# Modulation's first parts as six and two feature chunks, the first three units' products in another order, the input matrix turned later

## The chip, the cores and the metric

The kernel runs on one core of a Trainium2 chip, as one launch. Its time is the device time in microseconds (us), the median of several executions. All sizes are float32; the large products run as float32r, a form in which an operand is written as a high and a low part.

## The reference

Two transformer-like blocks over 512 tokens of 1024 features. The change touches only the beginning of the first block:

```python
def _rmsnorm(x, g):
    x32 = x.astype(jnp.float32)
    y = x32 * lax.rsqrt(jnp.mean(x32 * x32, axis=-1, keepdims=True) + EPS)
    return y.astype(x.dtype) * g
...
    c_act = jax.nn.silu(c)
    for l in range(DEPTH):
        mod = c_act @ w_ada[l] + b_ada[l]
        sh1, sc1, gt1, sh2, sc2, gt2 = jnp.split(mod, 6, axis=-1)
        u = _modulate(h, g_mix[l], sh1, sc1)
...
    proj = u @ w_in
    q, k, v, us, g_att, g_ssm = jnp.split(
        proj, [ATT_WIDTH, 2 * ATT_WIDTH, 3 * ATT_WIDTH, 3 * ATT_WIDTH + SSM_WIDTH,
               3 * ATT_WIDTH + SSM_WIDTH + D_MODEL], axis=-1)
```

The modulation vector `mod` is a product of one row with a 1024 x 6144 matrix. Its first two parts, the shift and the scale, are needed before the normalized input u can be formed, and u before any product with `w_in`. The state space branch (`us`) takes two of the first column blocks of `proj`; its input matrix B is scaled and grown over four steps before it is used. The rest of the reference, attention over three windows, gates, feed-forward parts and the whole second block, is the same before and after and does not bear on the change.

## The kernel before, in words

Activations lie transposed: 128 features on the partitions, 512 tokens along the row, so 1024 features are eight chunks. A **unit** is one block of 128 output columns: a weight tile of 128 x 1024 is loaded into `raw`, ScalarE (ACT) writes its high part `w_hi`, GpSimd (POOL) its low part `w_lo` (raw minus high), and TensorE (PE) makes for each of the eight chunks three products of 128x512 into one bank: high weights by high input, high weights by low input, low weights by high input, 24 in all. Two such buffers, s = 0 and 1, alternate for the whole kernel. ACT may refill a buffer's high part only when PE has signalled the end of the last unit that read it (`unit_done`); POOL follows ACT; PE waits for POOL (`lo_ready`).

Every engine runs a program written out by hand, in order, with semaphores between them; there is no scheduler. SyncE (SP) issues the loads.

The beginning goes like this. SP loads the columns, x, a table, then the first part of w_ada (shift and scale of chunks 0 to 3: eight loads of 512 KB, one for each 128 rows), three weight tiles of w_in, the second part (chunks 4 to 7), and so on. PE makes eight dummy products, then `ada_part(0, k)`: four quarter-array products for each of the eight loads, with dummy products (`keep_warm`) and two small sums for the norm between them. ACT copies the row out (`take_row`), PE turns it to columns (`turn_ada`), VectorE (DVE) makes shift and gain of four chunks (`take_half`), and then chunk by chunk: DVE scales x (`modulate`), ACT adds the shift and rounds (`shifted`, giving `u_hi`), DVE makes the rest (`shift_lo`, giving `u_lo`).

The first three units are not made one after the other, but grouped by chunk: `group_high`, `group_rest` and `group_low` are the three kinds of product for unit s and chunk c. Unit 2 has a place of its own (`third_raw`, `third_hi`, `third_lo`), units 0 and 1 use the two buffers. The second part's `ada_part(1, k)` stands between their products. After chunks 0 to 3 of all three come chunks 4 to 7 of units 0 and 1, then those of unit 2. Then PE turns the grown B matrix by 16 transposes of 128x128 (line 1068), which ACT copies out (line 1457), and the regular units begin with `in_unit` on buffer 1.

DVE grows B (`power_of_lam`, `grow`) between the first and second halves of its modulation, and POOL doubles a table of angles (`double`, `square_angle`) partly before, partly behind its first three splits. `ada_first` says where the parts of w_ada lie.

## Time and profile before

| | us |
|---|---|
| median of 3 runs | 2468.82 (2468.78 to 2470.03) |
| the profiled execution, its own time | 2468.61 |
| its span | 2466.8 |
| PE busy | 2453.8 (99% of the span) |
| DVE, POOL, ACT busy | 1168.4, 1070.8, 914.3 |

The page's first part gives busy time for each engine. PE is busy nearly throughout, in part with dummy products. The chain of waits says what released what. The timeline gives start, duration and form of instructions in order of time, rows of one form merged; the bracket at its end is the idle time before the row and what ended it. A row of PE with `x8` for four float32 products counts each twice; a float32r product counts once. The ends of matmuls are modelled and overlap the next start, so distances from start to start are what a stretch of products costs.

### The profile page before, as it was taken

Reading aid. Unit: us, or ns where it says so; the run is one execution under the profiler, and the core shown is the slowest. Engines: PE = TensorE matmul, PEld = TensorE weight load, DVE = VectorE, ACT = ScalarE, POOL = GpSimd, SP = SyncE. Lnnn points to the kernel's source line nnn. Section 1 sums busy time; section 2 is a strip of 40 time slices with the busy share of each in tenths; the row PEclk is TensorE's granted clock in tenths of the full one; section 3 lists DMA queues with packets and bytes.
Section 4 is the critical chain, followed back from the end, with each engine's and each line's share of the span. In section 5 each row is a group of like instructions: output and inputs, shape, how many; then the busy total and the mean of one; then the engine's idle time right before and its main releaser. Section 6 shows DMA issues by size and latency. Waiting matters only on the chain.

```text
span 2466.8 us, 32936 instructions
## 1 busy us (share of the span) xinstructions
PE 2453.8 (99%) x11477; PEld 2005.9 (81%) x11477; DVE 1168.4 (47%) x1728; ACT 914.3 (37%) x1307; POOL 1070.8 (43%) x529
## 2 busy tenths in 40 slices
PE   9999999999999999999999999999999999999999
PEld 6877888888888888877888888888888777888887
DVE  7574867256331345676330345331345666431332
ACT  4444443235322334555321334321234554431332
POOL 5332454444444445334444445444445334443444
PEclk9999999999999999999999999999999999999999
DMA  6223653332233331322232332233231332232332
GB/s 254 87 75 98 225 180 114 114 97 85 85 103 104 100 101 61 103 77 94 83 108 99 100 101 71 85 106 107 94 110 61 92 88 94 77 103 92 94 107 81
DMA packets 74062, 253.47 MB, mean 103 GB/s; under 512 B 9184, under 2 KB 13408, under 8 KB 73856
## 3 DMA queue, kind: packets, MB, share of 16 engines
q1 hardware_dynamic: 73408, 251.93, 31.6%
q8 instruction: 46, 0.75, 0.1%
q10 hardware_dynamic: 576, 0.52, 0.1%
q14 instruction: 32, 0.26, 0.0%
HBM read 244.76 MB, written 2.10 MB: 100 GB/s over the span
## 4 chain that ended last, share of the span: by engine, by line
PE 84%; issue 9%; DVE 3%; POOL 3%; ACT 1%; DMA 0%; SPq 0%; POOLq 0%; DVEq 0%; ACTq 0%
PE unit_bank L671 25%; PE unit_bank L673 25%; PE unit_bank L672 25%; POOL w_lo L530 2%; PE score L779 2%; PE score L769 1%; DVE arena L1772 1%; PE mix L672 1%; PE mix L673 1%; PE mix L671 1%; PE mix L927 1%; PE out_bank L906 1%; PE out_bank L726 0%; DVE arena L2521 0%; PE mix L1005 0%
## 5 line engine op out<-in xcount | busy, mean ns | idle before, releaser
L530 POOL TENSOR_TENSOR w_lo<-raw,w_hi 128x1024 fp32r<-128x1024 f32 (+2 forms) x374 | 953.8, 2550 | 1295.5 <-ACT w_hi L1268 1295.4
L1268 ACT ACTIVATE w_hi<-raw 128x1024 fp32r<-128x1024 f32 (+2 forms) x375 | 416.5, 1111 | 1163.9 <-PE unit_bank L673 1122.0
L671 PE MATMUL unit_bank<-u_hi,w_hi 128*128 128x512 f32 x2142 | 840.9, 393 | 0.4 <-POOL w_lo L530 0.4
L673 PE MATMUL unit_bank<-u_hi,w_lo 128*128 128x512 f32 x2142 | 835.2, 390 | 0.0
L672 PE MATMUL unit_bank<-u_lo,w_hi 128*128 128x512 f32 x2142 | 835.1, 390 | 0.0
L671 PEld LDWEIGHTS unit_bank<-u_hi,w_hi 128*128 128x128 f32 x2142 | 402.4, 188 | 93.6 <-issue 9.5
L673 PEld LDWEIGHTS unit_bank<-u_hi,w_lo 128*128 128x128 f32 x2142 | 402.4, 188 | 84.0
L672 PEld LDWEIGHTS unit_bank<-u_lo,w_hi 128*128 128x128 f32 x2142 | 402.6, 188 | 81.8 <-issue 0.2
L671 PE MATMUL unit_bank<-h_hi,w_hi 128*128 128x512 f32 x915 | 357.6, 391 | 0.2 <-DVE h_lo L2200 0.2
L673 PE MATMUL unit_bank<-h_hi,w_lo 128*128 128x512 f32 x915 | 356.6, 390 | 0.0
L672 PE MATMUL unit_bank<-h_lo,w_hi 128*128 128x512 f32 x915 | 356.6, 390 | 0.0
L2433 DVE TENSOR_TENSOR arena<-unit_bank,rstd 128x512 f32<-128x512 f32 x84 | 58.1, 691 | 398.9 <-PE unit_bank L673 398.9
L2442 DVE TENSOR_TENSOR h_lo<-arena,h_hi 128x512 f32 (+1 forms) x88 | 170.8, 1941 | 78.5 <-ACT h_hi L1641 78.5
L671 PEld LDWEIGHTS unit_bank<-h_hi,w_hi 128*128 128x128 f32 x915 | 171.9, 188 | 36.5 <-DVE h_lo L2200 0.7
L672 PEld LDWEIGHTS unit_bank<-h_lo,w_hi 128*128 128x128 f32 x915 | 171.9, 188 | 36.0 <-issue 0.5
L673 PEld LDWEIGHTS unit_bank<-h_hi,w_lo 128*128 128x128 f32 x915 | 171.9, 188 | 35.6
L2430 DVE TENSOR_TENSOR arena<-unit_bank,rstd 128x512 f32<-128x512 f32 x84 | 58.1, 692 | 138.8 <-PE unit_bank L673 138.8
L2344 DVE COPY f<-unit_bank 128x512 f32 (+1 forms) x43 | 29.7, 691 | 180.3 <-PE unit_bank L673 178.8
L1641 ACT ACTIVATE h_hi<-arena 128x512 f32 (+1 forms) x88 | 55.6, 632 | 33.9 <-DVE arena L2440 33.4
L2440 DVE TENSOR_TENSOR arena<-arena 128x512 f32<-128x512 f32 x88 | 60.9, 692 | 3.3
L2340 DVE TENSOR_TENSOR f<-unit_bank,f 128x512 f32 (+1 forms) x28 | 19.3, 689 | 80.4 <-PE unit_bank L673 79.4
L1636 ACT ACTIVATE arena<-arena 128x512 f32<-128x512 f32 x88 | 54.1, 615 | 2.9 <-DVE arena L2430 2.9
(422 smaller groups left out, 2176.7 us busy)
## 6 DMA issues: line engine op xcount, KB each, us to landing
raw<-in_w_gate_up SPq DMA_DIRECT2D x168, 512.0 KB, 3.5
raw<-in_w_down SPq DMA_DIRECT2D x64, 704.0 KB, 4.1
raw<-in_w_in SPq DMA_DIRECT2D x65, 512.0 KB, 3.5
raw<-in_w_up SPq DMA_DIRECT2D x30, 512.0 KB, 3.5
f<-in_w_ada_rows SPq DMA_DIRECT2D x26, 512.0 KB, 4.8
raw<-in_w_out SPq DMA_DIRECT2D x24, 512.0 KB, 3.6
raw<-in_w_down SPq DMA_DIRECT2D x16, 512.0 KB, 3.5
ada_in_u<-in_w_ada SPq DMA_DIRECT2D x8, 512.0 KB, 11.2
```

Source lines behind the costliest of these rows:

```text
L530: e.tensor_tensor(w_lo[:, s, 0:n], raw[:, s, 0:n], as32(w_hi[:, s, 0:n]), ALU.subtract).then_inc(lo_ready, 1)
L671: e.matmul(bank[:], wh, hi(k), start=begin and n == 0, stop=False)
L672: e.matmul(bank[:], wh, lo(k), start=False, stop=False)
L673: mm = e.matmul(bank[:], wl, hi(k), start=False, stop=end and last)
L779: e.matmul(score[s][:], w[:, s, c * P:(c + 1) * P], u_hi[:, c, :], start=c == 0 and w is first_hi, stop=False)
L1268: e.activation(w_hi[:, s, 0:n], raw[:, s, 0:n], ACT.Copy).then_inc(hi_ready, 1)
L1636: e.activation(ffn_s, ffn_g, ACT.Silu).then_inc(silu_ready, 1)
L1641: e.activation(h_hi[:, bass.ds(i, 1), :].rearrange("p a t -> p (a t)"), ffn_h, ACT.Copy).then_inc(hhi_ready, 1)
L2430: g = e.tensor_tensor(ffn_g, banks[0][:], rstd[:], ALU.mult)
L2433: u = e.tensor_tensor(ffn_u, banks[1][:], rstd[:], ALU.mult)
L2440: e.tensor_tensor(ffn_h, ffn_s, ffn_u, ALU.mult).then_inc(hidden_ready, 1)
L2442: e.tensor_tensor(flat(h_lo[:, bass.ds(i, 1), :]), ffn_h, as32(flat(h_hi[:, bass.ds(i, 1), :])), ALU.subtract).then_inc(h_ready, 1)
```

## The change

1. w_ada's first two parts are cut as six and two chunks instead of four and four. `FIRST_BLOCKS` gives the blocks of 128 columns per quarter (3 and 1, before 2 and 2), `FIRST_AT` the first chunk (0 and 6). The loads are 768 KB and 256 KB instead of twice 512 KB, eight of each as before. The loop with dummy products has 3 dummies at five places instead of 2 at six, and 10 instead of 12 behind the row's turn.
2. PE's order in the first three units: chunks 0 to 5 in one loop, in which unit 2's high and rest products and unit 0's low ones follow three chunks behind; then the rest of part 1, unit 1's and unit 2's low products; then chunks 6 and 7, unit 2's among them.
3. DVE makes all its modulation first and grows B behind it; PE's 16 transposes stand behind the first regular unit, ACT's four copies of them behind the copy of k.
4. POOL makes all its doublings before its first split.

```diff
+FIRST_BLOCKS, FIRST_AT = (3, 1), (0, 6)
...
-            def load_ada_first(half, loaded):
-
+            def load_ada_first(part, loaded):
+
+                at, n = FIRST_AT[part] * P, 2 * FIRST_BLOCKS[part] * P
                 for k in range(DC):
-                    src = d["w_ada"][k].rearrange("p (t c) -> p t c", t=2)[:, :, half * T:half * T + T]
-                    e.dma_start(ada_first[half][k].rearrange("p (t c) -> p t c", t=2), src).then_inc(loaded[k], 16)
+                    src = d["w_ada"][k].rearrange("p (t c) -> p t c", t=2)[:, :, at:at + n]
+                    e.dma_start(ada_first[part][k].rearrange("p (t c) -> p t c", t=2), src).then_inc(loaded[k], 16)
...
-            for n in (1, 2):
+            for n in (1, 2, 4, 8):
                 double(n)
                 square_angle()
+            e.sem_inc(turn_ready, 1)
             split_pair(IN1, D)
             e.wait_ge(hi_ready, 3)
             e.tensor_tensor(third_lo[:], third_raw[:], as32(third_hi[:]), ALU.subtract).then_inc(lo_ready, 1)
-            e.wait_ge(B_padded, 1)
-            for n in (4, 8):
-                double(n)
-                square_angle()
-            e.sem_inc(turn_ready, 1)
...
-                if k == 3:
+                if k == 4:
...
-                else:
-                    keep_warm(2)
-            turn_ada(0, score[0], 2)
-            keep_warm(12, out_bank)
-            for s in range(2):
-                e.wait_ge(hi_ready, s + 1)
-                e.wait_ge(taken[s], 1)
+                elif k < DC - 1:
+                    keep_warm(3)
+            turn_ada(0, score[0], FIRST_BLOCKS[0])
+            keep_warm(10, out_bank)
...
+            def third(c):
+
+                group_high(2, c)
+                group_rest(2, c)
+
...
+            first = FIRST_AT[1]
+            for c in range(first):
                 both(group_high, c, uhi_ready)
                 if c:
                     both(group_rest, c - 1, u_ready)
-                ada_part(1, c)
...
+                if c >= 2:
+                    ada_part(1, c - 2)
+                if c >= 3:
+                    e.wait_ge(lo_ready, 1)
+                    group_low(0, c - 3)
+                    e.wait_ge(hi_ready, 3)
+                    third(c - 3)
+            both(group_rest, first - 1, u_ready)
+            for k in range(first - 2, DC):
+                ada_part(1, k)
+            for c in range(first - 3, first):
+                group_low(0, c)
+                third(c)
+            turn_ada(1, score[0], FIRST_BLOCKS[1])
+            e.wait_ge(lo_ready, 2)
+            for c in range(first):
+                group_low(1, c)
             e.wait_ge(lo_ready, 3)
...
+            for c in range(first):
                 group_low(2, c)
...
+            for c in range(first, DC):
                 both(group_high, c, uhi_ready)
                 both(group_low, c)
-                if c > 4:
+                if c > first:
                     both(group_rest, c - 1, u_ready)
+                    third(c - 1)
             both(group_rest, DC - 1, u_ready, True)
-            for c in range(4, DC):
-                group_high(2, c)
-                group_rest(2, c)
+            third(DC - 1)
+            for c in range(first, DC):
                 group_low(2, c, c == DC - 1)
...
                 in_unit(in_pair(j, 0), 1)
                 if j:
                     turn_both(j - 1, 3)
+                else:
+                    turn_inputs()
...
                 e.activation(k_st, unit_bank[1][:], ACT.Copy).then_inc(taken[1], 1)
+                if j == 0:
+                    copy_turned()
...
-            modulate(range(4))
+            modulate(range(FIRST_AT[1]))
+            take_half(1)
+            modulate(range(FIRST_AT[1], DC))
             power_of_lam(2, 2)
             e.wait_ge(zeroed, 1)
             grow(B_grown, STRIDE, b_bar[:, 0, :, :], b_bar[:, 1, :, :], False)
             e.sem_inc(B_padded, 1)
-            take_half(1)
-            modulate(range(4, DC))
```

PE, the end of the first three units, before: `unit_bank` rows are units 0 and 1 (x2 for one product of each), `score` rows with `third_` names are unit 2, and the first `in_unit` follows.

```order
59 L713 MATMUL unit_bank<-u_hi,w_lo 128x512 x2
60 L706 MATMUL unit_bank<-u_lo,w_hi 128x512 x4
61 L701 MATMUL score<-u_hi,third_hi 128x512
62 L706 MATMUL score<-u_lo,third_hi 128x512
...
71 L706 MATMUL score<-u_lo,third_hi 128x512
72 L713 MATMUL score<-u_hi,third_lo 128x512
73 L1068 MATMUL score<-tabs,arena 128x128 x4
74 L1068 MATMUL mix<-tabs,arena 128x128 x8
75 L1068 MATMUL out_bank<-tabs,arena 128x128 x4
76 L671 MATMUL unit_bank<-u_hi,w_hi 128x512
```

The same place on PE now, up to the first `in_unit`, whose three kinds of product are lines 669 to 671.

```order
61 L699 MATMUL score<-u_hi,third_hi 128x512
62 L704 MATMUL score<-u_lo,third_hi 128x512
63 L704 MATMUL unit_bank<-u_lo,w_hi 128x512 x2
64 L699 MATMUL score<-u_hi,third_hi 128x512
65 L704 MATMUL score<-u_lo,third_hi 128x512
66 L711 MATMUL score<-u_hi,third_lo 128x512 x2
67 L669 MATMUL unit_bank<-u_hi,w_hi 128x512
```

Between the last product on units 0 and 1 and the first `in_unit` stood twelve products of unit 2 and 16 transposes; now four products stand there.

POOL, the doublings (`ssm_tmp`, `turn`, `angle`) around the first splits (`w_lo`, `third_lo`), before:

```order
24 L544 TENSOR_TENSOR angle<-angle 128x8 x5
25 L530 TENSOR_TENSOR w_lo<-raw,w_hi 128x1024 x2
26 L584 TENSOR_TENSOR third_lo<-third_raw,third_hi 128x1024
27 L544 TENSOR_TENSOR ssm_tmp<-turn,angle 128x32 x2
...
36 L544 TENSOR_TENSOR angle<-angle 128x8 x5
37 L591 TENSOR_TENSOR w_lo<-raw,w_hi 128x1024
```

POOL now:

```order
24 L546 TENSOR_TENSOR angle<-angle 128x8 x5
25 L546 TENSOR_TENSOR ssm_tmp<-turn,angle 128x32 x2
...
34 L546 TENSOR_TENSOR angle<-angle 128x8 x5
35 L532 TENSOR_TENSOR w_lo<-raw,w_hi 128x1024 x2
36 L587 TENSOR_TENSOR third_lo<-third_raw,third_hi 128x1024
37 L589 TENSOR_TENSOR w_lo<-raw,w_hi 128x1024
```

Ten rows of doublings have moved from behind the first three splits to ahead of them.

## Rows read from the trace of the kernel before

**Rows 1.** The page: busy time, share and instructions of each engine.
```profile
PE 2453.8 (99%) x11477; PEld 2005.9 (81%) x11477; DVE 1168.4 (47%) x1728; ACT 914.3 (37%) x1307; POOL 1070.8 (43%) x529
```

**Rows 2.** Timeline of PE: start us, us, engine, line, operation.
```profile
4.03 10.05 PE L1005 MATMUL mix<-cols 128*128 128x512 f32 x16 [4.03 <-DMA cols<-in_cols]
14.01 0.64 PE L976 MATMUL out_bank<-ada_in_u,c_act 128*32 128x256 f32 x8
14.58 0.71 PE L721 MATMUL score<-tabs 128*128 128x128 f32 x4
...
18.21 1.16 PE L726 MATMUL score<-tabs,arena 128*128 128x128 f32 x8
...
23.37 0.64 PE L976 MATMUL out_bank<-ada_in_u,c_act 128*32 128x256 f32 x8
...
24.80 2.84 PE L721 MATMUL out_bank<-tabs 128*128 128x128 f32 x24
27.46 0.70 PE L701 MATMUL unit_bank<-u_hi,w_hi 128*128 128x512 f32 x2
```

**Rows 3.** Timeline of ACT: refills of w_hi.
```profile
24.36 1.99 ACT L1268 ACTIVATE w_hi<-raw 128x1024 fp32r<-128x1024 f32 x2
...
47.95 1.06 ACT L1268 ACTIVATE w_hi<-raw 128x1024 fp32r<-128x1024 f32 x1 [2.22 <-PE unit_bank L706]
...
59.91 1.06 ACT L1268 ACTIVATE w_hi<-raw 128x1024 fp32r<-128x1024 f32 x1 [5.73 <-DMA raw<-in_w_in]
```

**Rows 4.** Timeline of SP: issues of part 0 and of unit 2's weights.
```profile
2.16 8.94 SPq L388 DMA_DIRECT2D ada_in_u<-in_w_ada  x8
...
12.96 0.61 SPq L395 DMA_DIRECT2D third_raw<-in_w_in  x1
```

**Rows 5.** DMA: first load of part 0, unit 2's load: us from issue to landing.
```profile
ada_in_u<-in_w_ada SPq DMA_DIRECT2D x1, 512.0 KB, 9.4
...
third_raw<-in_w_in SPq DMA_DIRECT2D x1, 512.0 KB, 13.3
```

**Rows 6.** Stretches of 2 us: busy by engine, clock, DMA share, GB/s.
```profile
6.00:8.00 2.00, 2.00 (x4) 0.92 (x3) 1.50 (x9) 0.20 (x1) 0.00 (x0) 1.00 1.00 418
...
16.00:18.00 2.00, 2.00 (x24) 1.15 (x23) 1.93 (x4) 0.00 (x0) 1.82 (x3) 1.00 1.05 386
```

**Rows 7.** Timeline of POOL, first splits, last doubling, fourth split.
```profile
25.55 4.71 POOL L530 TENSOR_TENSOR w_lo<-raw,w_hi 128x1024 fp32r<-128x1024 f32 x2 [2.88 <-ACT w_hi L1268]
...
39.60 0.56 POOL L544 TENSOR_TENSOR ssm_tmp<-turn,angle 128x32 f32<-128x32 f32 x2 [6.99 <-DVEq L1942]
...
45.23 1.32 POOL L544 TENSOR_TENSOR angle<-angle 128x8 f32<-128x8 f32 x5
49.09 2.41 POOL L591 TENSOR_TENSOR w_lo<-raw,w_hi 128x1024 fp32r<-128x1024 f32 x1 [2.54 <-ACT w_hi L1268]
```

**Rows 8.** Timeline of PE around the first three units' middle and end.
```profile
37.48 1.05 PE L976 MATMUL out_bank<-arena,c_act 128*32 128x256 f32 x16
38.45 0.50 PE L701 MATMUL score<-u_hi,third_hi 128*128 128x512 f32 x1
...
46.82 1.09 PE L706 MATMUL unit_bank<-u_lo,w_hi 128*128 128x512 f32 x4
...
50.49 0.60 PE L1068 MATMUL score<-tabs,arena 128*128 128x128 f32 x4
...
52.15 0.47 PE L671 MATMUL unit_bank<-u_hi,w_hi 128*128 128x512 f32 x1
...
57.72 0.39 PE L671 MATMUL unit_bank<-u_hi,w_hi 128*128 128x512 f32 x1
```

**Rows 9.** PE's waits from 60 us, longest group: us, times, longest.
```profile
PE out_bank L726 <- DVEq L2319: 1.0, 5, 0.2
```

**Rows 10.** Timeline of DVE: growing of B begins, scan's first.
```profile
31.82 1.02 DVE L1772 TENSOR_TENSOR co<-lam 128x8 f32<-128x8 f32 x2
...
68.63 0.42 DVE L1992 TENSOR_TENSOR ssm_tmp<-turn,f 128x256 f32<-128x256 f32 x1 [7.20 <-ACT f L1493]
```

More of the change, by code:

```diff
@@ L208, in program @@
         ada_in_f = f.rearrange("p (n c) t -> p n (c t)", c=4)
[L209 to L210 removed]
+        ada_first = [[ada_in_u[:, k, :] for k in range(5)] + [ada_in_h[:, k, :] for k in range(3)],
+                     [slot(12 + k) for k in range(DC)]]
         ada_gate = f.rearrange("p (n c) t -> p n (c t)", c=2)
         ada_shift = [ada_late[:], ada_in_f[:, 0, :], ada_in_f[:, 1, :]]
[L213 removed]
+        ada_row = [slot(20)[:, 0:3 * P], slot(20)[:, 3 * P:4 * P], slot(22)]
         gate_sum, shift_sum, gate2_sum = slot(20, 2), slot(18, 4), slot(24, 2)
@@ L970, in mixer2, with ada_part @@
                 norm(3 * l + 2, ffn2(l, 1) + 1)
-            def ada_part(half, k):
-                e.wait_ge((second_loaded if half else ada_loaded)[k], 16)
+            def ada_part(part, k):
+                n = FIRST_BLOCKS[part] * P
+                e.wait_ge((second_loaded if part else ada_loaded)[k], 16)
                 for q in range(4):
-                    mm = e.matmul(out_bank[32 * q:32 * q + 32, 0:2 * P], c_act[:, k:k + 1].broadcast_to([P, 32]),
-                                  ada_first[half][k][:, 2 * P * q:2 * P * (q + 1)], start=k == 0, stop=k == DC - 1)
+                    mm = e.matmul(out_bank[32 * q:32 * q + 32, 0:n], c_act[:, k:k + 1].broadcast_to([P, 32]),
+                                  ada_first[part][k][:, n * q:n * (q + 1)], start=k == 0, stop=k == DC - 1)
                 mm.then_inc(ada_used, 1)
@@ L1032, in both @@
                     product(s, c, last) if last else product(s, c)
-            for c in range(4):
+            def third(c):
+                group_high(2, c)
+                group_rest(2, c)
+            for s in range(2):
+                e.wait_ge(hi_ready, s + 1)
+                e.wait_ge(taken[s], 1)
+            first = FIRST_AT[1]
+            for c in range(first):
                 both(group_high, c, uhi_ready)
@@ L1037, in _ @@
                     both(group_rest, c - 1, u_ready)
-                ada_part(1, c)
-            both(group_rest, 3, u_ready)
-            for s in range(2):
-                e.wait_ge(lo_ready, s + 1)
-                for c in range(4):
-                    group_low(s, c)
-                ada_part(1, 4 + s)
-            ada_part(1, 6)
-            ada_part(1, 7)
+                if c >= 2:
[5 more added lines that the diff above has]
+                    third(c - 3)
@@ L1047, in _ @@
+            both(group_rest, first - 1, u_ready)
[8 more added lines that the diff above has]
+                group_low(1, c)
             e.wait_ge(lo_ready, 3)
-            for c in range(4):
-                group_high(2, c)
-                group_rest(2, c)
+            for c in range(first):
@@ L1437, in _ @@
             e.activation(third_hi[:], third_raw[:], ACT.Copy).then_inc(hi_ready, 1)
-            for c in range(2, 4):
+            for c in range(2, FIRST_AT[1]):
                 shifted(0, c)
-            take_row(2 * DC, 1, out_bank[:, 0:2 * P])
-            for c in range(4, DC):
+            take_row(2 * DC, 1, out_bank[:, 0:FIRST_BLOCKS[1] * P])
+            for c in range(FIRST_AT[1], DC):
                 shifted(1, c)
@@ L1454, in _, with copy_turned @@
             stage_q(group_bank[2])
-            for n, bank in enumerate((score[0], *mix, out_bank)):
-                e.wait_ge(B_turned, n + 1)
-                e.activation(slot(12 + n), bank[:], ACT.Copy).then_inc(B_ready, 1)
+            def copy_turned():
+                for n, bank in enumerate((score[0], *mix, out_bank)):
+                    e.wait_ge(B_turned, n + 1)
+                    e.activation(slot(12 + n), bank[:], ACT.Copy).then_inc(B_ready, 1)
             def gate(s, g):
@@ L1905, in take_half @@
             def take_half(half):
+                at, blocks = FIRST_AT[half], FIRST_BLOCKS[half]
                 def of_half(ap):
-                    return ap.rearrange("p (h q b) -> p h q b", h=2, q=2)[:, half, :, :]
-                turned = score[0][:, 0:2 * P].rearrange("p (b t q r) -> p t q b r", b=2, t=2, q=2)[:, :, :, :, 0]
-                amplified = score[0][:, 2 * P:2 * P + 8]
+                    return ap[:, at:at + 2 * blocks].rearrange("p (q b) -> p q b", q=2)
+                turned = score[0][:, 0:blocks * P].rearrange("p (b t q r) -> p t q b r", b=blocks, t=2, q=2)[:, :, :, :, 0]
+                amplified = score[0][:, 3 * P:3 * P + 8]
                 e.wait_ge(mod_turned, half + 1)
```

31 lines of the change are left out of this document (12 added, 19 removed).

## The prediction

> **What bounds the kernel now.** I read the page's busy times first: PE holds 2453.8 of 2466.8 us [rows 1], so only what delays or spares PE can move the end. Next the waits of PE behind 60 us: the longest of seven groups is 1.0 us in five pieces, and the seven add up to 3.9 [rows 9]. Nothing downstream has slack to give, and nothing there is touched: if the second regular unit starts d later, the kernel ends d later. That unit starts at 57.72 [rows 8]. So the question is where this mark goes.
>
> Three stretches lead to it. First product: at 27.46, right behind the dummies [rows 2]. From there to the first regular unit at 52.15 are 24.7 us. Then 24 products to 57.72, 5.57 us, or 0.23 us each [rows 8].
>
> **The beginning: six chunks' columns in part 0.** A piece takes 0.57 us from its start at 14.01 to the dummies' at 14.58; two dummies show 0.71 and the sums 1.16, which without the overlap of 0.07 that the piece shows too (0.64 against 0.57) is 0.64 and 1.09 [rows 2]; I give the norm's spread, of the same form and count, 1.09 as well. Two pieces in a row take 0.97, from 37.48 to 38.45 [rows 8], so about 0.49 is the flow of 256 columns and the rest is restarting. For 384 columns I scale 0.43 of the 0.57 by 1.5 (0.57 less 0.14 for starting): 0.78. Dummies cost 0.22 each (twelve from 24.80 to 27.46 [rows 2]), so three cost 0.87. The path on PE from 14.01: 8 x 0.78 + 5 x 0.87 + 2 x 1.09 = 12.8, so the last piece ends at 26.8. Before, it started at 23.37 and ended at 24.0. That is 2.8 later. If a piece did not grow with its width at all, it would end at 8 x 0.57 + 4.35 + 2.18 = 11.1, at 25.1; if all 0.57 grew, at 27.4.
>
> Are the loads earlier than that? The first load was issued at 2.2 [rows 4] and took 9.4 to land [rows 5], so 11.6. It carries 512 KB of the queue; at 386 GB/s [rows 6] 1.36 us. With 768 KB, the eighth lands at 11.6 + 0.7 + 7 x 2.04 = 26.5 by the rate of w_ada's stretch, and at 25.5 by the 418 GB/s of x's, whose rows are longer [rows 6]. PE starts its last piece at 26.0, so loads and PE are nearly tied; I take PE's 26.8 and keep 27.3 as the upper end.
>
> The Trainium skill speaks of this ("DMA: Bandwidth & Descriptors", Where 436 GB/s comes from): for a load from HBM to SBUF it lets the HBM side bind at about 358 GB/s for a core. The rows above disagree, with 386 and 418, and the measurement decides. By the page's figure, an estimate from it would put the eighth load at 27.7 and the end 1.2 us above my sum.
>
> From the last piece to the first product, the path before was 24.0 to 27.46: ACT's copy, PE's turn, three small steps of DVE, scaling, shift; ACT put its two refills, 1.99 together, between [rows 2, 3]. Now the copy has 384 columns instead of 256 (+0.1), the turn three blocks instead of two (+0.1). ACT's two refills need the tiles of w_in, which are queued behind part 0 and so land up to 1.3 and 2.6 us after 25.5 to 26.5: 27 and 28.3 in the middle. The copy ends at 27.3, refills end 28.3 and 29.3, and scaling is ready at 29.4: tied again. First product at 30.2, which is **+2.7**. With the slow loads it is 31.
>
> **The middle: the first three units.** All products stay: 72. Before: 24.7 us held 72 x 0.23 = 16.4, the eight pieces 4.6, 16 transposes 1.66 (50.49 to 52.15) [rows 8], and 2.0 of restarts and waits. Now: 16.4 for the products; pieces of 128 columns, by the same split, 0.35 each, of which four alone cost 0.45 with the restart and four in a row 0.3: 3.0; 0.2 for the turn; 0.6 at chunk 2, where ACT rounds unit 2's weights (third_raw landed at 12.96 + 13.3 = 26.3 before [rows 4, 5], and now at about 31) ahead of u_hi of chunk 2; 0.9 for some ten restarts of 0.1. That is 21.1 to the end of the first three units, at 51.3. DVE's second take_half is covered: its turn stands at 44.4, and 12 low products (2.7 us) lie over the 2.4 us of turn, scaling and shift.
>
> POOL's last doublings, 39.60 to 46.55, now stand before its splits, behind the earlier ones that ended at 22.7 (25.55 less 2.88 of waiting) [rows 7]: they end near 29.7, the first split at 32.1 and unit 0's low products start near 35. They cost nothing. In exchange POOL loses its 6.99 us wait for DVE [rows 7], which cost nothing either. If this cover went (35 against 32.1), each us above 2.9 would be paid.
>
> **The new wait.** Regular unit 3 uses buffer 1. Its high part can be written only when units 0 and 1 are done. Before, their last products began at 46.82 (four: 0.93), ACT wrote from 47.95 to 49.01, POOL from 49.09 to 51.50 [rows 3, 7, 8]; PE meanwhile had 12 products and 16 transposes, 4.4 us, and started at 52.15 without a wait. Round trip: 51.5 - 47.75 = 3.75. Now PE has four products, 0.9 us. It waits **2.8**. Behind the waiting product stands all of PE. Units 0 and 1 end at 50.4 (51.3 - 0.9), so unit 3 starts at 54.1.
>
> From the first product to unit 3 that is 23.9 instead of 24.7: **-0.8**. The new order buys 3.6 (24.7 - 21.1) and gives 2.8 back.
>
> **Behind unit 3.** The 16 transposes are no longer under POOL's split, but after the unit: **+1.7**, at 59.7 to 61.4. DVE's growing of B begins some 16 us later (31.82 before [rows 10]) and takes 7.8 us, as it released POOL at 39.60 [rows 7, 10], to about 55.4: ready before 59.7. The scan's preparation behind it ends near 70, and the scan waited 7.20 us for ACT until 68.63 [rows 10], which will now be near 71: the cover shrinks to about 1 us. What is queued behind ACT's four B copies (2.5 us) is a refill that waited for its load anyway. But these copies now follow the refill that waited 5.73 us for a load until 59.91 [rows 3]. That load is issued in the midst of SP's small copies, started by ACT's copies of units 0 and 1, 2.6 us later now: 62.5. Refill, copy of k and four B copies end at 66.6, and PE wants them at 61.4 + 5.5 = 66.9. A tie; I put **+0.1** and keep 0 to 1.
>
> **Sum:** 2.7 - 0.8 + 1.7 + 0.1 = +3.7. The profiled execution took 2468.61, 1.8 around its span, so 2472.3; the median of the runs lies 0.2 higher, so **2472.5**.
>
> **The rivals.**
> *The clock falls (slower still).* PE would idle 2.8 us at 51.3, with shorter gaps at 31. The granted clock is 1.00 in the stretches shown [rows 6], PE being always fed. Against: no row here shows a fall after an idle stretch, and nothing but that speaks for it. Price: the eight first products took 10.05 [rows 2] where, by the dummies of 128 columns at 0.22, they would take 7.0 (8 x 4 x 0.22), so 3.0 more. It gives 2475.5. The Trainium skill ("TensorE: Matmul & The Clock Gate", Part 1) has such a fall to half rate after idling; the gap here is short for its rule. No row here shows which.
>
> *Loads bind.* The w_ada loads run at 386 or slower, w_in's second tile lands at 29 or later, third_raw at 32: first product at 31 to 31.5, and the wait at chunk 2 grows by 1. The sum becomes 2.7 + 1.0 + 1.0 - 0.8 + 1.7 + 0.6 = +6.2: 2475.0. For it: the queue is full, at a share of 1.00 and more [rows 6]; against: packets grow from 2 to 3 KB.
>
> *Nothing is lost: later waits absorb it (not slower).* If PE's waits behind 60 us are for engines that do not follow PE, being late would shorten them. All seven groups are 3.9, so with all of them the time is 2468.8 or a little less. It decides once nearly all of the 3.7 is taken up. Against: those waits are round trips that PE starts itself (the longest is DVE's, in pieces of 0.2) [rows 9], which move along.
>
> *The pieces do not grow and the part is bound by ACT.* Then the first product is at 29.4 and the middle shorter by 0.7: +2.2, 2471.0. Likely enough to be part of my own range.
>
> **How the numbers follow.** My forecast, 2471 to 2474: 0.62. Pieces cheap: 0.12, 2470 to 2471. Loads bind: 0.12. Clock falls: 0.08. Absorbed: 0.04. Something larger in favour: 0.02. A measurement can tell about 0.2%, 4.9 us, so below 2463.9 is faster and above 2473.8 slower. Slower takes both slow rivals (0.20) and the top of my own range (0.05), 0.25; faster 0.02; the same 0.73. The range of 8 in 10 is 2470.0 to 2475.6.
>
> **What would show it.** In the new timeline: last piece of part 0 ends at 26.8 (24.0 before), first product at 30.2, PE idle about 2.8 us before the first regular unit with POOL as releaser, that unit at 54.1, transposes behind it, second regular unit at 61.4. Wrong if that idle time is missing or under 2, if the first product comes before 29, or if the second unit's shift (3.7) differs from the shift of the whole time by more than 0.5.

## The result and the profile after

The changed kernel takes 2475.88 us, the median of 9 runs (2474.24 to 2477.38); the kernel before takes 2468.78 (9 runs, 2468.54 to 2470.03). The ratio is 1.0029, 95% interval 1.0020 to 1.0037: 7.1 us slower, where 3.7 were forecast. The profiled execution took 2475.65 us with a span of 2473.9. The nine executions are not alike: in one the mean granted clock over the whole span is 1.000, and it took 2474.24; in the other eight it is 0.999 or 0.998, and they took 2475.58 to 2477.38. Some 3.4 us at half speed lower that mean by 0.0007, so 0.999 fits one such stretch and 1.000 none. The profiled one is of the eight.

The page of the changed kernel, its busy time of PE (busy us, share of the span, instructions):

```profile
PE 2455.5 (99%) x11479; PEld 2005.5 (81%) x11479; DVE 1171.9 (47%) x1728; ACT 914.6 (37%) x1307; POOL 1072.0 (43%) x529
```

PE is busy 1.7 us longer than before [rows 1] with two instructions more, although every product takes as long at full clock as it did. So part of the 7.1 us are products that ran slower, and most of the rest is PE standing still.

PE's waits over the whole kernel (who, whose work it waited for: us in total, times, longest):

```profile
PE mix L1004 <- DMA cols<-in_cols: 4.1, 1, 4.1
PE unit_bank L669 <- POOL w_lo L589: 3.2, 1, 3.2
PE out_bank L975 <- DMA ada_in_h<-in_w_ada: 1.0, 1, 1.0
PE out_bank L724 <- DVEq L2341: 1.0, 5, 0.2
...
PE unit_bank L699 <- ACT u_hi L1422: 0.8, 2, 0.5
PE score L983 <- ACT arena L1442: 0.6, 1, 0.6
```

The first was there before [rows 2], and so were the 1.0 in five pieces [rows 9] and others like it. New are the 3.2 for POOL, 1.0 for a load of part 0 and 0.6 for ACT's copy; the wait for u_hi was 0.3 before and is 0.8 in two pieces.

The timeline of PE to the first products, with their line numbers of the changed kernel (start us, us, engine, line, operation, and in brackets the idle time before it and its releaser); it answers to [rows 2]:

```profile
13.77 0.85 PE L975 MATMUL out_bank<-ada_in_u,c_act 128*32 128x384 f32 x8
14.55 0.94 PE L719 MATMUL score<-tabs 128*128 128x128 f32 x6
15.42 0.85 PE L975 MATMUL out_bank<-ada_in_u,c_act 128*32 128x384 f32 x8
...
24.89 0.94 PE L719 MATMUL score<-tabs 128*128 128x128 f32 x6
26.84 0.85 PE L975 MATMUL out_bank<-ada_in_h,c_act 128*32 128x384 f32 x8 [1.01 <-DMA ada_in_h<-in_w_ada]
28.30 0.55 PE L983 MATMUL score<-tabs,arena 128*128 128x128 f32 x3 [0.61 <-ACT arena L1442]
28.68 2.40 PE L719 MATMUL out_bank<-tabs 128*128 128x128 f32 x20
31.36 1.30 PE L699 MATMUL unit_bank<-u_hi,w_hi 128*128 128x512 f32 x4 [0.28 <-ACT u_hi L1422]
```

A piece takes 0.78 (13.77 to 14.55) and three dummies 0.87, both as forecast. But the last piece waits 1.0 for its load, and the first product is at 31.36: 3.90 later than before, not 2.7.

The same timeline where the first three units end, answering to [rows 8]:

```profile
51.98 0.61 PE L711 MATMUL score<-u_hi,third_lo 128*128 128x512 f32 x2
55.78 0.50 PE L669 MATMUL unit_bank<-u_hi,w_hi 128*128 128x512 f32 x1 [3.18 <-POOL w_lo L589]
...
57.31 0.63 PE L669 MATMUL unit_bank<-u_hi,w_hi 128*128 128x512 f32 x1
57.73 0.63 PE L670 MATMUL unit_bank<-u_lo,w_hi 128*128 128x512 f32 x1
...
60.68 0.39 PE L671 MATMUL unit_bank<-u_hi,w_lo 128*128 128x512 f32 x1
...
62.98 0.60 PE L1080 MATMUL score<-tabs,arena 128*128 128x128 f32 x4
...
64.65 0.48 PE L669 MATMUL unit_bank<-u_hi,w_hi 128*128 128x512 f32 x1
```

The first regular unit starts at 55.78 after the wait of 3.18. Its first six products take 1.5 us, to 57.31; there they begin to follow each other at 0.43 us, and from 60.68 on ten products take 2.3, at 0.23 each again. The stretches of 4 us, and one of 1 us inside the slow part, say why (window; length; busy us and instructions of PE, PEld, DVE, ACT, POOL; the granted clock as a share of 2.4 GHz; DMA share; GB/s):

```profile
52.00:56.00 4.00, 0.82 (x4) 0.40 (x3) 3.90 (x4) 3.19 (x5) 3.13 (x2) 1.00 0.05 11
56.00:60.00 4.00, 4.00 (x13) 3.11 (x13) 3.90 (x4) 0.00 (x0) 2.52 (x1) 0.65 0.25 54
60.00:64.00 4.00, 4.00 (x23) 3.37 (x22) 3.48 (x13) 0.44 (x1) 0.00 (x0) 0.92 0.57 172
...
58.00:59.00 1.00, 1.00 (x3) 0.72 (x3) 1.00 (x1) 0.00 (x0) 0.52 (x1) 0.50 0.18 39
```

In the first, PE stood still for 3.2 us; behind it the granted clock is 0.65 and then 0.92. From 58 to 59 us it is 0.50: the products that follow each other at twice the distance ran at the level of 1.2 GHz. Unit 3 and the transposes take 8.87 us (55.78 to 64.65); at full clock they took 5.57 and 1.66 before [rows 8], 7.23.

The second regular unit starts at 64.65, 6.93 later than before, and the profiled executions differ by 7.04. So the whole loss lies ahead of this mark: +3.90 to the first product, -0.27 from there to unit 3 (24.42 instead of 24.69), +1.66 for the transposes' place and +1.64 for the clock.

POOL and DVE, each engine's own timeline around that wait; POOL's first row answers to the split in [rows 7]:

```profile
52.87 2.85 POOL L589 TENSOR_TENSOR w_lo<-raw,w_hi 128x1024 fp32r<-128x1024 f32 x1 [15.88 <-ACT w_hi L1283]
55.69 2.83 POOL L532 TENSOR_TENSOR w_lo<-raw,w_hi 128x1024 fp32r<-128x1024 f32 x1
```

```profile
53.55 5.52 DVE L1792 TENSOR_TENSOR arena<-arena,lam 128x512 f32<-128x512 f32 x2
59.10 1.41 DVE L1792 TENSOR_TENSOR arena<-arena 64x512 f32<-64x512 f32 x2
```

POOL's split took 2.85 instead of 2.41, and two operations of DVE, which elsewhere in the growing of B take 1.42 together, took 5.52. DVE grows B later now, and meets POOL's splits there. This is not in the prediction at all.

### The profile page after: what moved, and what is told of

Same layout as the page of the kernel before. It is cut to its first block, busy times and chain, and to the rows that moved or that the text cites. A ratio compares the mean times of both kernels' runs of the same rounds, so it can differ in the third digit from the quotient of the medians.

```text
span 2473.9 us, 32939 instructions
## 1 busy us (share of the span) xinstructions
PE 2455.5 (99%) x11479; PEld 2005.5 (81%) x11479; DVE 1171.9 (47%) x1728; ACT 914.6 (37%) x1307; POOL 1072.0 (43%) x529
## 4 chain that ended last, share of the span: by engine, by line
PE 83%; issue 9%; POOL 3%; DVE 3%; ACT 1%; DMA 0%; SPq 0%; POOLq 0%; DVEq 0%; ACTq 0%
PE unit_bank L669 25%; PE unit_bank L670 25%; PE unit_bank L671 25%; POOL w_lo L532 2%; PE score L777 2%; PE score L767 1%; PE mix L671 1%; PE mix L670 1%; PE mix L669 1%; PE mix L925 1%; PE out_bank L904 1%; PE out_bank L724 0%; DVE arena L2543 0%; DVE arena L1792 0%; PE mix L933 0%
```

## The experiments

All times are medians of 7 to 11 runs of a kernel, beside runs of the kernel before on the same chip (2468.52 to 2468.66 us); differences are against those, unless the changed kernel is named: that one is the result above, 2475.88, from other executions. The 95% interval of a ratio is some 2 us to either side, so a difference of 1 to 2 us between two kernels rests on what their traces show at the place, and not on the medians alone.

**The clock: dummies in the wait.** Thirteen dummy products on PE between the last products of unit 2 and unit 3, in the changed kernel:

```diff
             for c in range(first, DC):
                 group_low(2, c, c == DC - 1)
+            keep_warm(13, out_bank)
```

> The changed kernel with 13 dummy products of 128x128 between the last product of unit 2 and the first regular unit (0.22 us each, 2.9 us in a gap that showed 3.2). Theory A (the clock falls because PE idles there, and costs 8.87 - 7.23 = 1.6 us behind the gap, on top of the wait): granted clock 1.00 throughout 56 to 64 us, unit 3 and the transposes back at 7.2 us, time 2475.9 - 1.6 = 2474.3. Theory B (the slow stretch has another cause, for instance GpSimd and VectorE disturbing each other at the same place): stretch and time as in the changed kernel, 2475.9.

Measured: 2474.34 (2473.92 to 2475.74), ratio 1.0023 [1.0014, 1.0033], 1.5 us less than the changed kernel. PE does more work, starts unit 3 0.3 later and comes to the second regular unit at 63.36, 1.3 sooner. Its timeline in the gap, and one stretch of 4 us:

```profile
52.72 3.06 PE L719 MATMUL out_bank<-tabs 128*128 128x128 f32 x26
56.07 0.50 PE L669 MATMUL unit_bank<-u_hi,w_hi 128*128 128x512 f32 x1 [0.29 <-POOL w_lo L589]
```

```profile
56.00:60.00 4.00, 3.93 (x17) 3.23 (x18) 3.93 (x3) 0.00 (x0) 2.82 (x2) 1.00 0.22 49
```

The same window has four products more and a clock of 1.00. So the slow products came from PE's idling, and they cost about 1.6 us: eight products at 0.43 in place of 0.23. The executions say the same. Here eight of ten have a mean clock of 1.000, against one of nine for the changed kernel, and that one's 2474.24 is the time that the fed gap gives.

**The wait: unit 2's products kept back.** In the changed kernel, unit 2's high and rest products of chunks 3 to 7 are moved behind the last products of units 0 and 1, so twelve products stand there instead of four (the text below counts 18, 4.1 us; there are ten high and rest products and two low ones, 2.7 us):

```diff
             for c in range(first - 3, first):
                 group_low(0, c)
-                third(c)
...
-                    third(c - 1)
             both(group_rest, DC - 1, u_ready, True)
-            third(DC - 1)
+            for c in range(first - 3, DC):
+                third(c)
```

> The changed kernel with unit 2's high and rest products of chunks 3 to 7 moved behind the last products of units 0 and 1, so that 18 products (4.1 us) and not 4 (0.9 us) lie over ScalarE's refill and GpSimd's split for unit 3. Theory A (the wait of 3.2 us is the round trip without cover, and the slow clock follows from it): both go, unit 3 starts at about 52.9 instead of 55.8, time 2475.9 - 2.9 - 1.6 = 2471.4; if VectorE's growing of B (ready at 60.5) is then late for the transposes at 58.5, up to 2.0 of it comes back, 2473.4. Theory B (the time is lost ahead of the first product and behind the first regular unit only): no more than 1 us changes.

Measured: 2472.39 (2471.76 to 2473.22), ratio 1.0015 [1.0006, 1.0025]: +3.8, which is 3.3 less than the changed kernel's 7.1. The wait is not gone:

```profile
54.07 0.50 PE L669 MATMUL unit_bank<-u_hi,w_hi 128*128 128x512 f32 x1 [1.11 <-POOL w_lo L589]
```

From the end of units 0 and 1 at 50.08 to unit 3 are 3.99 us, the round trip, and twelve products cover 2.7 of them; that leaves the 1.1. Behind it the clock stayed at 1.00. So the products' order explains most of the wait of 3.2 and the clock behind it, 3.3 of the 7.1 us together. What is left, 3.8, is near the 3.9 of the first product.

This profiled execution has a fall of the clock at another place. Ahead of its first product PE waited 1.39 for part 0's last load and 0.61 for ACT's copy, with one piece between, and the ten dummies behind that took 3.61 us instead of 2.7:

```profile
29.01 3.86 PE L719 MATMUL out_bank<-tabs 128*128 128x128 f32 x20
32.62 1.18 PE L699 MATMUL unit_bank<-u_hi,w_hi 128*128 128x512 f32 x4
```

```profile
30.00:31.00 1.00, 1.00 (x7) 1.00 (x6) 0.95 (x2) 0.69 (x2) 1.00 (x1) 0.50 1.09 350
```

The run with the fed gap waited there for 1.43 and 0.61 and kept 1.00. So waits of nearly the same length are followed by a fall in one execution and by none in another.

**Loads and parts alone.** The kernel before with parts of six and two chunks (buffers, loads, pieces, DVE's two halves), unit 2's products, the growing of B and the transposes in the old places, and ten dummies for twelve behind the turn, as in the changed kernel:

```diff
+FIRST_BLOCKS, FIRST_AT = (3, 1), (0, 6)
...
-        ada_in_h = in_h("ada_in_h", 5, [6, D])
+        ada_in_h = in_h("ada_in_h", 5, [3, 3 * T])
...
-            modulate(range(4))
+            modulate(range(6))
             power_of_lam(2, 2)
             e.wait_ge(zeroed, 1)
             grow(B_grown, STRIDE, b_bar[:, 0, :, :], b_bar[:, 1, :, :], False)
             e.sem_inc(B_padded, 1)
             take_half(1)
-            modulate(range(4, DC))
+            modulate(range(6, DC))
```

> The kernel before with w_ada's parts as six and two chunks and the old order of the rest as far as it goes (chunks 0 to 5 of units 0 and 1, then unit 2's chunks 0 to 3, then chunks 6 and 7, then unit 2's chunks 4 to 7; growing of B between VectorE's two modulations; transposes ahead of unit 3). Theory A (the larger part 0 delays the first product by 3.9 us whatever follows): first product near 31.4, no wait of 3 us ahead of unit 3 and no fall of the clock; a wait for chunk 6, since VectorE grows B ahead of it, of up to 3 us; time 2468.8 + 3.9 = 2472.7, 1 to 2 more or less by that wait and by the narrower pieces. Theory B (only the new order costs): under 2470.

Measured: 2472.14 (2471.51 to 2474.21), ratio 1.0015 [1.0006, 1.0025]: +3.6. The first product is at 31.45, 3.99 later than before, and unit 3 at 55.44, 3.29 later, with a clock of 1.00 throughout. So 0.7 of what the start loses is given back behind it, and the rest stays.

**The order alone.** The changed kernel with two halves of four chunks, loaded as before, and everything else new:

```diff
-FIRST_BLOCKS, FIRST_AT = (3, 1), (0, 6)
+FIRST_BLOCKS, FIRST_AT = (2, 2), (0, 4)
...
-        ada_in_h = in_h("ada_in_h", 5, [3, 3 * T])
+        ada_in_h = in_h("ada_in_h", 5, [6, D])
...
-                    keep_warm(3)
+                    keep_warm(2)
```

> The changed kernel with the modulation parts loaded as two halves of four chunks again, everything else new (unit 2's products between those of units 0 and 1, growing of B behind all of the modulation, transposes behind the first regular unit, POOL's doublings ahead of its first split). Theory (loads and pieces cost 3.6 to 3.9 us by themselves, order, transposes and the clock the other 3): first product back at 27.5, and 2471.5 to 2472.0 with a wait of 3 us for POOL ahead of unit 3 and a clock below 1.00 behind it. Rival (with the first product early and the loads of w_in landing no sooner, the wait ahead of unit 3 stays under 3 us and the clock holds): 2469.7. Rival (the two parts of the change need each other, as six chunks modulated in one go feed the new order and four do not): 2474 or more, with PE waiting for ACT's u_hi.

Measured: 2473.04 (2471.26 to 2473.74), ratio 1.0016 [1.0007, 1.0025]: +4.4, between what the theory and the second rival said. The first product is back at 27.39. Unit 3, and the clock behind it:

```profile
53.37 0.80 PE L669 MATMUL unit_bank<-u_hi,w_hi 128*128 128x512 f32 x1 [2.31 <-POOL w_lo L589]
```

```profile
52.00:56.00 4.00, 2.63 (x6) 2.15 (x7) 3.97 (x2) 1.20 (x2) 4.00 (x2) 0.65 0.18 39
56.00:60.00 4.00, 4.00 (x18) 3.19 (x18) 3.62 (x9) 0.00 (x0) 0.09 (x1) 0.93 0.45 139
```

Here the clock falls with a wait of only 2.3, where the first rival had it hold under 3. It is down when PE resumes: unit 3's first products already follow each other at 0.4 to 0.6. Unit 3 is 1.2 late, the transposes cost 1.7 and the clock 1.5, 4.4 in all. Eight of the eleven executions have a mean clock of 0.999 (2472.46 to 2473.74), the other three 1.000 (2471.26 to 2471.61): the clock falls in most executions of this kernel and not in all (only the profiled one shows its waits). So even with the old loads the new order does not gain. The two halves of the change cost 3.6 and 4.4 alone and 7.1 together; the 0.9 between is less than these runs can tell from nothing.

**PE's own path or the loads.** The changed kernel with one dummy behind a piece of part 0 in place of three:

```diff
                 elif k < DC - 1:
-                    keep_warm(3)
+                    keep_warm(1)
```

> The changed kernel with one dummy product instead of three at five places ahead of part 0's last piece: PE's own path to the last piece is 10 x 0.22 = 2.2 us shorter. Theory A (the last piece waits for its load, as the 1.0 us wait in the trace says): it still starts at 26.8 and the time stays 2475.9. Theory B (PE's own path sets it, as the prediction's sum had it): the first product comes 1 to 2 us earlier, time 2474. A third: the PE idles 3 us in all ahead of 26.8 and the clock may fall there, which would make it slower by up to 1.6.

Measured: 2476.16 (2474.16 to 2477.77), the same as the changed kernel. PE is through earlier, and it makes no difference, because ACT waits for the next loads. The last piece starts at 25.99 and not at 26.8 as expected; it still waits for its load, 0.70, but that load landed sooner in this execution. ACT's timeline, first in the changed kernel, then in this one (copy of the row, the two refills, u_hi):

```profile
27.75 0.49 ACT L1442 ACTIVATE arena<-out_bank 128x384 f32<-128x384 f32 x1 [5.16 <-PE out_bank L975]
28.14 1.05 ACT L1283 ACTIVATE w_hi<-raw 128x1024 fp32r<-128x1024 f32 x1
29.37 1.06 ACT L1283 ACTIVATE w_hi<-raw 128x1024 fp32r<-128x1024 f32 x1 [0.18 <-DMA raw<-in_w_in]
30.53 1.35 ACT L1422 ACTIVATE u_hi<-mix,mod 128x512 fp32r<-128x512 f32 x2
```

```profile
26.91 0.49 ACT L1442 ACTIVATE arena<-out_bank 128x384 f32<-128x384 f32 x1 [4.58 <-PE out_bank L975]
28.45 1.06 ACT L1283 ACTIVATE w_hi<-raw 128x1024 fp32r<-128x1024 f32 x1 [1.05 <-DMA raw<-in_w_in]
29.73 1.06 ACT L1283 ACTIVATE w_hi<-raw 128x1024 fp32r<-128x1024 f32 x1 [0.22 <-DMA raw<-in_w_in]
30.70 1.25 ACT L1422 ACTIVATE u_hi<-mix,mod 128x512 fp32r<-128x512 f32 x2
```

The copy comes 0.84 sooner, and the refills wait 1.05 and 0.22 for w_in's first two tiles, which stand in the queue behind part 0. The second tile is there at 29.37 in the one and 29.73 in the other; its refill ends some 1.06 later, and sets u_hi and with it the first product, at 31.51 here. Before, neither refill waited for a load [rows 3].

**The transposes alone.** The kernel before with PE's transposes of B behind the first regular unit and ACT's copies of them behind k:

```diff
                 if j:
                     turn_both(j - 1, 3)
+                else:
+                    turn_inputs()
...
                 e.activation(k_st, unit_bank[1][:], ACT.Copy).then_inc(taken[1], 1)
+                if j == 0:
+                    copy_turned()
```

> The kernel before with only the 16 transposes moved behind the first regular unit and ScalarE's four copies of them behind the copy of k. Theory A (they were free where they stood, as cover for GpSimd's split, and cost 1.66 us where they stand now): unit 3 starts at 51.6 instead of 52.15, the second regular unit 1.2 later, time 2470.0. Theory B (they cost the same anywhere): 2468.8. If ScalarE's copies come too late for the products on B, up to 1 us more.

Measured: 2469.71 (2469.47 to 2470.64), ratio 1.0005 [0.9996, 1.0014]: +1.1, with 1 inside the interval, though all eleven executions lie above the highest of the kernel before (2469.30). PE waits 0.9 for POOL instead of doing the transposes (1.66) there, and does them later, on its path.

**Unit 2's last products alone.** The kernel before with the high, rest and low products of unit 2's chunks 4 to 7 between those of units 0 and 1:

```diff
                 both(group_low, c)
+                group_low(2, c)
                 if c > 4:
                     both(group_rest, c - 1, u_ready)
+                    group_high(2, c - 1)
+                    group_rest(2, c - 1)
...
-            for c in range(4, DC):
-                group_high(2, c)
-                group_rest(2, c)
-                group_low(2, c, c == DC - 1)
+            group_high(2, DC - 1)
+            group_rest(2, DC - 1, True)
```

> The kernel before with unit 2's products of chunks 4 to 7 set between those of units 0 and 1, so that 2 products and the 16 transposes (2.1 us) lie over the refill and split for unit 3 instead of 12 and 16 (4.4 us). Theory A (a round trip of 3.75 us counts from the last product on units 0 and 1): unit 3 starts at 50.0 + 3.75 = 53.8, 1.6 later, time 2470.4, clock 1.00. Theory B (the order is free as long as PE makes as many products): 2468.8.

Measured: 2470.03 (2469.77 to 2470.41), ratio 1.0006 [0.9997, 1.0015]: +1.45, with the same reservation. The transposes cover the gap in part, PE waits 1.4, and the clock stays at 1.00.

**Both.** The two edits above in one kernel.

> Both together: the kernel before with the old loads, the interleaved end of unit 2 and the transposes behind unit 3. PE has 2 products (0.5 us) over the round trip of 3.75. Theory A: wait of 3.3 us, unit 3 at 53.8, the next unit 1.6 + 1.66 = 3.3 later, and, if the clock falls with a wait of this length as in the changed kernel, 1.6 more: 2473.7; without the fall 2472.1. This is then the part of the loss that the order makes alone.

Measured: 2473.16 (2471.74 to 2474.81), ratio 1.0019 [1.0010, 1.0028]: +4.6, where the two alone make 2.6. The wait is whole, and the clock pays:

```profile
52.00:56.00 4.00, 2.47 (x6) 1.99 (x7) 3.97 (x2) 1.45 (x3) 3.98 (x2) 0.62 0.15 33
```

PE waited 3.1 for POOL ahead of unit 3, at 53.53, and the clock was down when it resumed. Again this is so in most executions only: eight of the eleven have 0.999 (2473.11 to 2474.81), three have 1.000 (2471.74 to 2471.90). Two edits that each expose a part of one gap, and are cheap alone, together make it long enough for the slow clock in most executions.

**POOL's doublings alone.** The kernel before with POOL's doublings 4 and 8 ahead of its first split, as in the changed kernel:

```diff
-            for n in (1, 2):
+            for n in (1, 2, 4, 8):
                 double(n)
                 square_angle()
+            e.sem_inc(turn_ready, 1)
             split_pair(IN1, D)
...
-            e.wait_ge(B_padded, 1)
-            for n in (4, 8):
-                double(n)
-                square_angle()
-            e.sem_inc(turn_ready, 1)
```

> The kernel before with GpSimd's last doublings ahead of its first split. Theory A (free): 2468.8. The splits begin at 29.7 instead of 25.6, the low products of unit 0 wait for the first until 32.1 and stand at 34.3: no wait. Theory B (they are in the way of the splits): some tenths to 1 us slower, with a wait of PE for w_lo between 33 and 38 us.

Measured: 2474.65 (2473.47 to 2475.27), ratio 1.0024 [1.0015, 1.0034]: +6.1, nearly as much as the whole change. None of my theories had it. The timelines of POOL, of DVE, and PE's wait:

```profile
29.86 4.73 POOL L530 TENSOR_TENSOR w_lo<-raw,w_hi 128x1024 fp32r<-128x1024 f32 x2 [0.18 <-POOL angle L544]
34.56 2.38 POOL L585 TENSOR_TENSOR third_lo<-third_raw,third_hi 128x1024 fp32r<-128x1024 f32 x1
```

```profile
31.70 2.93 DVE L1768 TENSOR_TENSOR co<-lam 128x8 f32<-128x8 f32 x2
34.66 2.31 DVE L1768 TENSOR_TENSOR lam<-co 128x8 f32<-128x8 f32 x1
...
37.42 0.17 DVE L1768 TENSOR_TENSOR lam<-co 128x8 f32<-128x8 f32 x1
...
43.54 0.16 DVE L1910 TENSOR_TENSOR mod<-score,cols 128x4 f32<-128x4 f32 x1 [0.16 <-DVE arena L1768]
```

```profile
PE unit_bank L697 <- ACT u_hi L1403: 4.2, 1, 4.2
```

The splits, moved by the doublings, now run from 29.86 to 36.94, and DVE's first operations on lam, of which the same form takes 0.17 at 37.42, take 2.93 for two and 2.31 for one beside them and end where POOL's do: 34.63 and 36.97, POOL's 34.59 and 36.94. DVE comes to the second half of the modulation at 43.54, 3.9 later than before (39.67), and PE waits 4.2 for it. The granted clock behind that is 0.84 from 44 to 48 us and 0.73 from 48 to 52. The kernel before has such a meeting too, where nothing waits for it: beside POOL's split at 49.09 one DVE operation of 128x8, started at 49.19, took 2.32.

The Trainium skill ("SBUF — State Buffer", Who interferes with whom) says that VectorE and GpSimd share one pair of ports, an exclusive lock held for the whole instruction, and that a VectorE instruction with two inputs in SBUF contends with one of GpSimd that reads SBUF. The durations above agree: 0.17 became 2.31, and the operation ended with POOL's.

**The same, with DVE's growing out of the way.** As the last, and DVE grows B behind the second half's modulation, so that the transposes are late too:

```diff
             modulate(range(4))
+            take_half(1)
+            modulate(range(4, DC))
             power_of_lam(2, 2)
             e.wait_ge(zeroed, 1)
             grow(B_grown, STRIDE, b_bar[:, 0, :, :], b_bar[:, 1, :, :], False)
             e.sem_inc(B_padded, 1)
-            take_half(1)
-            modulate(range(4, DC))
```

> The kernel before with POOL's doublings ahead of its first split, as in the run that cost 6 us, but with DVE growing B behind the second half's modulation, and so the transposes behind the first regular unit and ACT's copies behind k. Theory (the 6 us came from POOL's splits holding up DVE's short operations ahead of the second half's modulation, for which PE waited): with growing out of that place PE's wait for u_hi goes, and the time is 2469.7 to 2471, the late transposes' price of 1.1 us and up to 1.5 for the wait ahead of unit 3. Rival (the later splits themselves hold up PE's low products, wherever DVE grows B): 2474 to 2476. If DVE's blocked operations merely move, w_lo of unit 3 lands as late as in the changed kernel, and PE waits 3 us there: 2472.

Measured: 2470.66 (2470.46 to 2471.25), ratio 1.0009 [1.0000, 1.0018]: +2.0. Of the 6.1 us 4.1 are gone though an edit that alone costs 1.1 was added: the loss had come through DVE's place, not through the late splits. The collision is now where the changed kernel has it:

```profile
49.27 5.72 DVE L1778 TENSOR_TENSOR arena<-arena 64x512 f32<-64x512 f32 x2
```

These are operations that take 1.41 for two when POOL rests. PE waits 0.9 for POOL ahead of unit 3, and 0.6 for B ahead of its transposes.

**Fewer dummies before.** The kernel before with one dummy in place of two behind each piece of the first half:

```diff
                 else:
-                    keep_warm(2)
+                    keep_warm(1)
```

> The kernel before, with one dummy product in place of two behind each modulation piece of the first half, so PE is through its own path sooner. Theory (in the old order PE's own path, not the loads, sets the first half's last piece): the pieces end up to 1.2 us sooner until the loads bind, 2467.5. Rival (the loads land barely ahead of PE, as they did behind the changed kernel's pieces): 2468.6, no change. A third: fewer dummies let the clock fall below full speed ahead of the first products, 2470 or more.

Measured: 2468.20 (2467.90 to 2468.80), ratio 0.9998 [0.9989, 1.0007]. The first product is at 27.00, 0.46 sooner and not the 1.2 expected, since PE now waits 1.1 for DVE's sums of x; the median is 0.46 lower, below what such runs can tell.

**Still fewer.** One behind each of the first three pieces, none behind the later:

```diff
-                else:
-                    keep_warm(2)
+                elif k < 3:
+                    keep_warm(1)
```

> The kernel before with one dummy product behind each of the first three pieces and none behind the later ones. With one everywhere the first product came 0.46 us sooner and the time fell by 0.4, the last three pieces running back to back behind PE's wait for the statistics of x. Theory (in the old order PE's own path, not the loads, sets the last piece; the last load lands at 21 to 22 us): the last piece ends another 0.8 us sooner, the first product is at 26.2, and the time is 2467.2 to 2467.6. Rival (ACT's copy of the row, its two refills and DVE's modulation behind it wait for the raw weights or for x0's root instead): 2468.2, as with one everywhere. Rival (PE's clock is let down by the holes between pieces): over 2469.

Measured: 2467.88 (2467.40 to 2469.19), ratio 0.9998 [0.9989, 1.0007]. The first product is at 25.85, 1.6 sooner than before, and then the loads show, in PE's timeline:

```profile
25.85 0.69 PE L701 MATMUL unit_bank<-u_hi,w_hi 128*128 128x512 f32 x2
27.29 0.64 PE L976 MATMUL out_bank<-ada_in_h,c_act 128*32 128x256 f32 x8 [0.75 <-DMA ada_in_h<-in_w_ada]
```

PE waits 0.75 for the second half's first piece. It is the lowest median of all, 0.6 below the kernel before, and not told apart from it.

## Why the prediction was right and wrong

The direction, the places and the kinds of wait were right; three terms were not, and the sum came out at 3.7 instead of 7.1. Two steps failed: the start went by PE's own path where the loads set it (1.2 short), and the clock's fall was put at nothing (1.64 short). The new wait was 0.5 short besides.

- **The beginning, +2.7 forecast, +3.90 measured.** The pieces (0.78) and dummies (0.87) were exact. The step that failed is "loads and PE are nearly tied; I take PE's 26.8": PE was ready for the last piece at 25.83, and the load landed at 26.84. The second tie of that section decided: the refills, put at 28.3 and 29.3, waited for w_in's tiles, and the second ended at 30.4. The run with fewer dummies shows that these tiles bind, and not the piece: its copy was 0.84 earlier, and the first product was no sooner. The tiles were put at 27 and 28.3, though the section's own 25.5 to 26.5 with 1.3 and 2.6 behind it has its middle at 27.3 and 28.6 and its late end at 29.1; the second was there at 29.37. I had that case as a rival, loads bind, first product at 31 to 31.5, at 0.12. Its other part, a longer pause at chunk 2, did not come, and its sum holds a further 0.6 that no sentence explains. The estimate by the slower rate has a slip too: a piece begun at 27.7 ends at 28.5, 1.7 above 26.8 and not 1.2.
- **The middle, -0.8 forecast, -0.27 measured.** The products and pieces took 21.07 us (31.36 to 52.43), as forecast (21.1). PE's wait for POOL was 3.18 and not 2.8, or 3.35 from start to start. Most of that 0.5 is POOL's split, 2.85 for 2.41, beside DVE's growing of B. That the growing lengthened it is likely and not shown: in the order alone the same split, beside the same growing, took 2.44. I moved that growing by 16 us (17.6 measured) and asked only whether it would be ready in time, not whom it would meet. The pause at chunk 2, 0.6 forecast, was 0.49.
- **The clock, 0 forecast, +1.64 measured.** "PE would idle 2.8 us" was priced at nothing, and its rival at 3.0 with a chance of 0.08. That the idling brings the fall is shown: with the gap fed by dummies or mostly covered by unit 2's products the clock there is 1.00, and with it open (the changed kernel, both edits, the order alone) it is 0.62 to 0.65 in a stretch of 4 us. It falls in most executions, not in all: in eight of nine of the changed kernel. The ninth, at 2474.24, lies inside the forecast's range. The price of 3.0 was read from the eight first products, about which the rows do not say that: the trace before has a granted clock of 1.00 in every microsecond from 4 to 14. A fall costs 1.3 to 1.6 here.
- **The transposes, +1.7 forecast, +1.66 measured.** In the kernel before alone they cost 1.1, since a part covered the wait there.
- **B's copies, +0.1 forecast:** the whole time moved by 7.04 where the mark moved by 6.93, so at most that. Right.
- **"They cost nothing", of POOL's doublings.** In the changed kernel no wait of PE's comes from the later splits directly. But the reason given, that the low products start late enough, was not the one that mattered. In the old order the same move costs 6.1. It does less harm here because DVE's growing moved as well, as the run with that growing out of the way shows (+2.0 in place of +6.1), and that puts the collision at 53 us. No run of the changed kernel leaves the doublings where they were, so what they cost in it is open.
- **"Not slower".** No wait behind 60 us shrank; the mark and the end moved together.

The range failed because two rivals, loads and clock, were priced as if only one could happen. They stand in different stretches and add: with the 1.2 of the one and the 1.6 of the other on 3.7, the sum is 6.5, and the 0.5 of the longer wait brings it to 7.0. Both had a chance of their own, and neither excluded the other.

Still open: what decides, at equal waits, whether the clock falls. Ahead of unit 3 it stayed at 1.00 in the traces with waits of 0.9, 1.1 and 1.4, and fell in those with 2.3, 3.1 and 3.2; but some executions of the same kernels kept it, by their mean clock, and one with two short waits in a row, ahead of the first product, lost it.

## What to carry to other kernels

A gap of PE's that another engine fills is priced by its length and by what the clock does behind it: here a wait of 2.3 to 3.2 us cost 1.3 to 1.6 more in most executions, and dummies in it gave that back. When two estimates are tied, take the later and add something, since an end at the later of two is never earlier than either; and rivals that stand in different stretches are added, not chosen between. Whoever moves work of GpSimd or VectorE asks what the other does at the new time, because a short operation there can take as long as the long one it meets.

## What the hardware showed that I had not expected

- DVE and POOL held each other up by far more than a share: two operations of DVE that take 1.42 us took 5.52 beside POOL's splits, one of 0.17 took 2.31, and POOL's split of 128x1024 went from 2.41 to 2.85.
- The clock fell with a single wait of 2.3 us in a kernel whose PE is busy 99% of the time. In the changed kernel it fell over a microsecond after PE had resumed (rate halved from 57.31, PE having resumed at 55.78) and was back at 60.68; in the order alone and with both edits it was down already when PE resumed.
- The same program kept its clock in some executions: one of nine of the changed kernel (2474.24, the others 2475.58 and more), three of eleven of the order alone and of both edits. The mean granted clock of each execution, 1.000 or 0.999, tells them apart.
